# One early Silu on ScalarE, and the sum over h's squares one unit earlier, in a transformer block

## The chip, the cores and the metric

The kernel runs on one core of a Trainium2 chip. Its time is the device time of one execution in microseconds (us), as the median of several runs. The profile is that of one execution; its times count from the start of the span.

## The reference

A transformer block for 256 tokens of width 2048: an RMS norm, a projection into two attention branches with gates, the branches and their output product, and then the part that matters here, the second RMS norm and a gated feed-forward of width 5632:

```python
h = h + merged @ w_out[l]
hn = rms_norm(h, norm_ffn_g[l])          # h * rsqrt(mean(h*h) + eps) * g
h = h + (jax.nn.silu(hn @ w_ffn_gate[l]) * (hn @ w_ffn_up[l])) @ w_ffn_down[l]
```

All tensors are float32.

## The kernel before

Every product is taken in three passes. A matrix is split into a high half (a rounded copy, made by ScalarE) and a low half (the rest, made by VectorE), and TensorE sums high x high, low x high and high x low (L1593 to L1595). The products therefore need three engines in turn for each piece of a weight: SP's queue loads it, ScalarE makes `u_hi` (`unit_hi`, L946), VectorE makes `u_lo` (`unit_lo`, L1292), and TensorE multiplies (`product`).

The last quarter of the output product and the whole feed-forward run in units. A unit is a 512 x 512 piece of a weight (or a sum of such pieces), and a panel is the work for one pair of column blocks. In a "gu" panel these are 512 columns of the gate's product and the same of the up product. The first 1024 rows of a panel are multiplied with seven products in place of eight (M1 to M7, with sums and differences of quarters that VectorE forms: `sum_p` L1299, `sum_r` L1304, `sum_z` L1308). The other rows are plain units N0 to N3. An M unit has 12 matmuls, and an N or O unit has 24 (12 for each half of the tokens). N0 and N1 belong to the gate's half, N2 and N3 to the up half. The order is written out by hand:

```python
FIRST_ORDER = ("O0", "O1", "M1", "O2", "M5", "O3", "M6", "M2", "M7", "N0", "M3", "N1", "M4")
ORDER = ("M1", "N2-", "M5", "N3-", "M6", "M2", "M7", "N0", "M3", "N1", "M4")
```

The first line is panel 0, the second every later panel; "N2-" is unit N2 of the panel before. All engines walk the same list. Each of ScalarE and VectorE does the half of the unit and then what `first_unit` (panel 0) or `next_unit` (later panels) puts behind that unit. The high halves have four slots, three while panel 0 runs, and the low halves have three, so a unit's half can be made only when TensorE has used an older one.

The second norm's factor, `h_rs`, is a number for each token. It isn't applied to h ahead of the products but to their sums: `gate_opened` (L960) is a Silu of a gate bank with `h_rs` as its scale. It is made in these steps:

- ScalarE squares each quarter of h with a sum over its columns (`squares_of`, L1017), which raises `h_ss_ready`. The last quarter's squares stand behind N0's high half.
- VectorE adds the four sums (L1394, into `h_sum`) behind M4's low half of panel 0.
- GpSimd makes mean plus eps (`h_ms`, L729) and the power -0.5 (`h_rs`, L730). Its queue has the store of h's last quarter ahead of them and `sum_q` of panel 1 behind them (L756, a transfer that adds one quarter of a weight to another).

ScalarE's `gate_opened(panel 0, 0)` stands behind the high half of N2 in panel 1. It waits for the bank's last product (N1's first half) and for `h_rs`. TensorE's unit M1 of panel 1 writes into that same bank, and so has three waits: for its low half, for `gate_ready`, and for the operand:

```python
pe.wait_ge(lo_ready, u.index + 1)
...
elif before.kind == "gu":
    pe.wait_ge(gate_ready, T * before.col + 1)
...
left_ready(panel, 0)
```

ScalarE's functions need a table; the program has a table load (ACT_TABLE_LOAD) where a function is not in the loaded one. In the source no load is written; they come with the compilation. The kernel uses Copy, Square, Exp, Sigmoid (L867, L868) and Silu.

Of the kernel before, what the change touches and what calls it, by code (L numbers as in the profile page):

```python
# [23 lines left out]
ACT = mybir.ActivationFunctionType  # L24
# [3 lines left out]
P = 128  # L28
# [253 lines left out]
def build(nc, x, norm_mix_g, w_in, q_norm_a, k_norm_a, sink_a, t5_bias, q_norm_b, k_norm_b, rel_bias_b,  # L282
# [4 lines left out]
    NB = D // COLS  # L287
# [22 lines left out]
    with ExitStack() as ctx:  # L310
# [3 lines left out]
        def take(nbytes):  # L314
            offset = top[0]
            top[0] += nbytes + (-nbytes) % 32
            return offset

        def at(name, shape, dt, offset):
            return nc.alloc_sbuf_tensor_at(name, shape, dt, offset=offset)  # L320

        def sb(name, shape, dt=F32):
            return at(name, shape, dt, take(int(np.prod(shape[1:])) * 4))
# [71 lines left out]
        ident = sb("ident", [P, P])  # L395
# [9 lines left out]
        h_ss = sb("h_ss", [P, T, NB])  # L405
        h_sum = sb("h_sum", [P, T])
        h_ms = sb("h_ms", [P, T])
        h_rs = sb("h_rs", [P, T])
        q_ss = sb("q_ss", [P, T * NH])
        q_ms = sb("q_ms", [P, T * NH])  # L410
# [137 lines left out]
        def groups(n):  # L548
            return bass.ds(n * GROUP, GROUP) if not isinstance(n, int) else slice(n * GROUP, (n + 1) * GROUP)
# [228 lines left out]
        def _(act):  # L778
            A = nc.scalar.activation
# [28 lines left out]
            def scaled_to_hi(n):  # L808
                act.wait_ge(scaled_ready, n + 1)
                ts = 1 if n == 0 else T  # L810
                A(xT_hi[:, groups(n), :].rearrange("p k (t s) -> p t k s", t=T)[:, 0:ts],
                  staged[:].rearrange("p t (k s) -> p t k s", k=GROUP)[:, 0:ts], ACT.Copy).then_inc(scaled_hi, 1)
# [121 lines left out]
            def unit_hi(u):  # L934

                panel, slot = u.panel, u.panel.slot[u.raw]
                if u.name in ("M5", "M6", "M4"):
                    act.wait_ge(sum_ready, sums(panel, {"M5": "P", "M6": "R", "M4": "Z"}[u.name]))
                elif u.name == "M7":
                    act.wait_ge(q_summed, 16 * (panel.n + 1))  # L940
                else:
                    act.wait_ge(quad_landed[slot], panel.landed[u.raw])
                act.wait_ge(piece_used, u.hi_after)
                if u.hi == HI_SLOTS - 1:
                    act.wait_ge(xT_ready, KT // PIECE_KT + NB)
                A(u_hi[u.hi][:], quad[slot][:], ACT.Copy).then_inc(hi_ready, 1)  # L946
# [33 lines left out]
            def copy_m5(panel):  # L980

                act.wait_ge(piece_used, panel.unit["M5"].index + 1)
                if panel.n:
                    act.wait_ge(e_seeded, panel.n)
                A(m5, by_group(e_bank(panel)[:]), ACT.Copy).then_inc(m5_copied, 1)

            def copy_m1(panel):

                act.wait_ge(piece_used, panel.unit["M1"].index + 1)
                before = panel.prev  # L990
                if before is None:
                    act.wait_ge(h_ready, NB - 1)
                elif before.kind == "gu":
                    act.wait_ge(gate_ready, T * (before.col + 1))
                else:
                    act.wait_ge(evacuated0, T * (before.down + 1))
                A(b_bank(panel)[:], a_bank(panel)[:], ACT.Copy).then_inc(m1_copied, 1)
# [16 lines left out]
            def squares_of(n):  # L1014
                act.wait_ge(h_ready, n + 1)
                for t in range(T):
                    A(side_b[:, t, :], h[:, t, columns_of(n)], ACT.Square,  # L1017
                      accum_out=h_ss[:, t, n:n + 1]).then_inc(h_ss_ready, 1)

            def first_unit(u):  # L1020

                panel = panels[0]
                if u.name == "M6":
                    copy_m1(panel)
                if u.name == "M7":
                    copy_m5(panel)
                unit_hi(u)
                if u.name == "M1":
                    squares_of(NB - 2)
                if u.name == "M6":  # L1030
                    scaled_to_hi(NB - 2)
                if u.name == "N0":
                    squares_of(NB - 1)
                if u.name == "M3":
                    scaled_to_hi(NB - 1)

            def next_unit(panel, u):

                before = panel.prev
                if u.name == "M6":  # L1040
                    copy_m1(panel)
                if u.name == "M7":
                    copy_m5(panel)
                unit_hi(u)
                own = u.panel is panel
                if before.kind == "gu":
                    if u.name == "N2" and not own:
                        gate_opened(before, 0)
                    if u.name == "M5":
                        gate_opened(before, 1)  # L1050
                    if u.name == ("N1" if "N1" in panel.unit else "M4"):
                        hidden_hi(before)
                    if u.name == "M4" and before.block_slot == 1:
                        forms_hi(before)
                else:
                    if u.name == "N2" and not own:
                        evacuate(before, 0, 0)
                    if u.name == "M5":
                        evacuate(before, 0, 1)
                    if u.name == "M4":  # L1060
                        evacuate(before, 1, 0)
                        evacuate(before, 1, 1)
# [9 lines left out]
        def _(dve):  # L1072
# [27 lines left out]
            def scale_h(n, sets):  # L1100

                dve.wait_ge(turned, sets)
                if n:
                    dve.wait_ge(xT_ready, KT // PIECE_KT + n)
                g0 = KT + n * GROUP
                for t in range(T):
                    ins = V.tensor_tensor(by_group(staged[:, t, :]), by_group(bank[T_BANK + t][:]),
                                          g_col[:, g0:g0 + GROUP, None].to_broadcast([P, GROUP, P]), ALU.mult)
                ins.then_inc(scaled_ready, 1)
# [21 lines left out]
            def add_to_h(j, ready):  # L1131
                for t in range(T):
                    ins = V.tensor_tensor(h[:, t, columns(j)], bank[2 * j.pair + t][:], h[:, t, columns(j)], ALU.add)
                ins.then_inc(ready, 1)
# [154 lines left out]
            def unit_lo(u):  # L1289
                dve.wait_ge(hi_ready, u.index + 1)  # L1290
                dve.wait_ge(piece_used, u.lo_after)
                V.tensor_tensor(u_lo[u.lo][:], quad[u.panel.slot[u.raw]][:], u_hi[u.hi][:].bitcast(F32),  # L1292
                                ALU.subtract).then_inc(lo_ready, 1)

            def sum_p(panel):

                dve.wait_ge(quad_landed[panel.slot["12"]], panel.landed["12"])
                dst = quad[panel.slot["11"]][:]
                V.tensor_tensor(dst, dst, quad[panel.slot["12"]][:], ALU.add).then_inc(sum_ready, 1)  # L1299

            def sum_r(panel):
                dve.wait_ge(quad_landed[panel.slot["22"]], panel.landed["22"])
                dst = quad[panel.slot["11"]][:]
                V.tensor_tensor(dst, dst, quad[panel.slot["22"]][:], ALU.add).then_inc(sum_ready, 1)  # L1304
# [62 lines left out]
            def first_unit(u):  # L1367

                panel = panels[0]
                unit_lo(u)  # L1370
                if u.name == "O1":
                    dve.wait_ge(piece_used, PIECES)
                    add_to_h(jobs[-1], h_ready)
                if u.name == "M1":
                    sum_p(panel)
                if u.name == "M5":
                    sum_r(panel)
                if u.name == "O3":
                    scale_h(NB - 2, SETS - 1)
                if u.name == "M6":  # L1380
                    scaled_to_lo(NB - 2)
                if u.name == "M2":
                    add_last_to_h()
                if u.name == "M7":
                    seed_c(panel)
                if u.name == "N0":
                    scale_h(NB - 1, SETS)
                if u.name == "M3":
                    seed_e(panel)
                    scaled_to_lo(NB - 1)  # L1390
                    sum_z(panel)
                if u.name == "M4":
                    dve.wait_ge(h_ss_ready, T * NB)
                    V.tensor_reduce(h_sum[:], h_ss[:], AX.X, ALU.add).then_inc(h_sum_ready, 1)  # L1394

# [355 lines left out]
```

## Time and profile before

| | |
|---|---|
| median of 3 runs | 1291.85 us (1291.83 to 1291.9) |
| the profiled execution | 1291.89 us |
| its span | 1290.0 us |
| granted TensorE clock | 1.0 |
| busy: TensorE, weight load, VectorE, ScalarE, GpSimd | 99%, 82%, 74%, 55%, 5% |

The profiled execution's own time is 1.9 us more than the span, which counts from its first to its last instruction. TensorE's busy time includes the overlap of pipelined matmuls, so its pace is read from the starts of matmuls one after the other.

### The profile page before, as it was taken

The numbers are of one execution on the slowest core, as the hardware profiler recorded it, in microseconds if no ns is written. First come the engines' busy times: TensorE is split into PE (matmuls) and PEld (weight loads), VectorE is DVE, ScalarE is ACT, GpSimd is POOL, SyncE is SP. The second block draws the span as 40 slices with busy tenths as digits, with TensorE's granted clock in tenths as the row PEclk, the third lists the DMA queues.
The fourth block names the chain that finished last, engine by engine and source line by source line (L and its number), as shares of the span: only waits on it lengthen the run. The fifth ranks groups of instructions, "written<-read, shape, count | busy, mean of one in ns | idle before, by whom it ended". The sixth has DMA issues, their size and how long they took to land.

```text
span 1290.0 us, 15328 instructions
## 1 busy us (share of the span) xinstructions
PE 1283.5 (99%) x5996; PEld 1057.3 (82%) x5996; DVE 952.7 (74%) x919; ACT 709.5 (55%) x768; POOL 66.4 (5%) x65
## 2 busy tenths in 40 slices
PE   9999999999999999999999999999999999999999
PEld 7888887777788888888888888888888888888887
DVE  5655656777554555667898988888898878788996
ACT  5644445666554444455666655565565555565653
POOL 1221200000000000000100000000000001000000
DMA  8655376444466555676866687887957698866874
GB/s 296 224 170 194 131 238 207 152 151 151 162 238 193 178 185 195 211 248 192 290 215 217 192 260 230 253 244 220 293 200 227 194 276 256 252 225 196 276 218 125
DMA packets 136722, 276.55 MB, mean 214 GB/s; under 512 B 5248, under 2 KB 13760, under 8 KB 134224
## 3 DMA queue, kind: packets, MB, share of 16 engines
q1 hardware_dynamic: 130624, 250.37, 56.1%
q0 software_dynamic: 6032, 25.26, 10.4%
q8 instruction: 45, 0.74, 0.2%
q14 instruction: 21, 0.17, 0.0%
HBM read 249.38 MB, written 8.41 MB: 200 GB/s over the span
## 4 chain that ended last, share of the span: by engine, by line
PE 98%; ACT 1%; DVE 1%; DMA 0%; issue 0%; SPq 0%; ACTq 0%
PE bank L1593 18%; PE bank L1595 18%; PE bank L1594 18%; PE bank L1544 13%; PE bank L1546 13%; PE bank L1545 13%; PE bank L1492 1%; PE bank L1477 1%; PE bank L1517 1%; PE bank L1625 1%; PE bank L1502 1%; DMA x_rows<-in_x 0%; DVE u_lo L1292 0%; ACT prob L895 0%; PE bank L1519 0%
## 5 line engine op out<-in xcount | busy, mean ns | idle before, releaser
L1292 DVE TENSOR_TENSOR u_lo<-quad,u_hi 128x2048 fp32r<-128x2048 f32 x187 | 424.7, 2289 | 88.4 <-PE bank L1595 47.5
L946 ACT ACTIVATE u_hi<-quad 128x2048 fp32r<-128x2048 f32 x187 | 355.6, 1915 | 229.4 <-PE bank L1595 142.0
L1086 DVE TENSOR_TENSOR w_lo<-raw,w_hi 128x1024 fp32r<-128x1024 f32 (+1 forms) x192 | 229.6, 1202 | 190.4 <-ACT w_hi L791 188.2
L791 ACT ACTIVATE w_hi<-raw 128x1024 fp32r<-128x1024 f32 (+1 forms) x192 | 199.7, 1042 | 248.2 <-PE bank L1546 246.5
L1544 PE MATMUL bank<-w_hi,xT_hi 128*128 128x512 f32 (+1 forms) x544 | 213.7, 393 | 0.0
L1546 PE MATMUL bank<-w_lo,xT_hi 128*128 128x512 f32 (+1 forms) x544 | 208.8, 384 | 0.0
L1545 PE MATMUL bank<-w_hi,xT_lo 128*128 128x512 f32 (+1 forms) x544 | 208.6, 383 | 0.0
L1593 PE MATMUL bank<-u_hi,xT_hi 128*128 128x512 f32 x484 | 188.4, 389 | 0.7 <-DVE u_lo L1292 0.7
L1595 PE MATMUL bank<-u_lo,xT_hi 128*128 128x512 f32 x484 | 188.3, 389 | 0.0
L1594 PE MATMUL bank<-u_hi,xT_lo 128*128 128x512 f32 x484 | 188.3, 389 | 0.0
L1544 PEld LDWEIGHTS bank<-w_hi,xT_hi 128*128 128x128 f32 x544 | 102.3, 188 | 22.0 <-issue 1.0
L1546 PEld LDWEIGHTS bank<-w_lo,xT_hi 128*128 128x128 f32 x544 | 102.2, 188 | 20.7
L1545 PEld LDWEIGHTS bank<-w_hi,xT_lo 128*128 128x128 f32 x544 | 102.4, 188 | 18.3
L1593 PEld LDWEIGHTS bank<-u_hi,xT_hi 128*128 128x128 f32 x484 | 90.9, 188 | 19.9 <-DVE u_lo L1292 1.1
L1595 PEld LDWEIGHTS bank<-u_lo,xT_hi 128*128 128x128 f32 x484 | 90.9, 188 | 18.8
L1594 PEld LDWEIGHTS bank<-u_hi,xT_lo 128*128 128x128 f32 x484 | 90.9, 188 | 18.8
L1595 PE MATMUL bank<-u_lo,fT_hi 128*128 128x512 f32 (+1 forms) x236 | 91.0, 385 | 0.0
L1594 PE MATMUL bank<-u_hi,fT_lo 128*128 128x512 f32 (+1 forms) x236 | 91.0, 385 | 0.0
L1593 PE MATMUL bank<-u_hi,fT_hi 128*128 128x512 f32 (+1 forms) x236 | 91.0, 385 | 0.0
L1593 PE MATMUL bank<-u_hi,xs_hi 128*128 128x512 f32 x176 | 69.3, 394 | 0.0
L1595 PE MATMUL bank<-u_lo,xs_hi 128*128 128x512 f32 x176 | 68.6, 390 | 0.0
L1594 PE MATMUL bank<-u_hi,xs_lo 128*128 128x512 f32 x176 | 68.5, 389 | 0.0
(175 smaller groups left out, 1570.6 us busy)
## 6 DMA issues: line engine op xcount, KB each, us to landing
raw<-in_w_in SPq DMA_DIRECT2D x60, 1024.0 KB, 5.4
quad<-in_w_ffn_gate SPq DMA_DIRECT2D x44, 1024.0 KB, 7.0
quad<-in_w_ffn_up SPq DMA_DIRECT2D x44, 1024.0 KB, 6.1
quad<-in_w_ffn_down SPq DMA_DIRECT2D x44, 1024.0 KB, 6.4
quad<-quad POOLq DMA_DIRECT2D x17, 1024.0 KB, 8.2
raw<-in_w_out SPq DMA_DIRECT2D x12, 1024.0 KB, 5.1
raw<-in_w_branch_a SPq DMA_DIRECT2D x8, 1024.0 KB, 5.1
raw<-in_w_branch_b SPq DMA_DIRECT2D x8, 1024.0 KB, 5.1
```

The source lines that it names most:

```text
L791: A(w_hi[:, p % SPLIT_SLOTS, 0:w], raw[:, c % RAW_SLOTS, (p % 2) * w:(p % 2 + 1) * w], ACT.Copy).then_inc(hi_ready, 1)
L946: A(u_hi[u.hi][:], quad[slot][:], ACT.Copy).then_inc(hi_ready, 1)
L1086: V.tensor_tensor(w_lo[:, p % SPLIT_SLOTS, 0:w], raw[:, p // 2 % RAW_SLOTS, (p % 2) * w:(p % 2 + 1) * w], w_hi[:, p % SPLIT_SLOTS, 0:w].bi ...
L1292: V.tensor_tensor(u_lo[u.lo][:], quad[u.panel.slot[u.raw]][:], u_hi[u.hi][:].bitcast(F32), ALU.subtract).then_inc(lo_ready, 1)
L1477: ins = turn(bank[T_BANK + t][:, g * P:(g + 1) * P], src[:, t, g * P:(g + 1) * P], ident[:])
L1492: ins = M(dst, qT[rows, b * PAIRS + n, tokens(t)], k, start=True, stop=True)
L1544: M(sums, x_hi, w_hi[:, p % SPLIT_SLOTS, w], start=kt == 0, stop=False)
L1545: M(sums, x_lo, w_hi[:, p % SPLIT_SLOTS, w], start=False, stop=False)
L1546: ins = M(sums, x_hi, w_lo[:, p % SPLIT_SLOTS, w], start=False, stop=kt == j.kts - 1)
L1593: M(sums, a_hi(k), hi[:, w], start=start and k == 0, stop=False, skip_group_check=True)
L1594: M(sums, a_lo(k), hi[:, w], start=False, stop=False, skip_group_check=True)
L1595: ins = M(sums, a_hi(k), lo[:, w], start=False, stop=k == UNIT_KT - 1, skip_group_check=True)
```

## The change

ScalarE gets one more activation in `first_unit`, behind the high half of M3 and the copy of h's last transposed quarter: a Silu over four columns of the constant tile `ident` into a new tile `h_warm` that nothing reads. VectorE's sum over the four sums of squares, with its wait, moves from behind M4's low half to behind N1's, one unit earlier. The computed values are the same.

```diff
@@ -405,6 +405,7 @@
         h_ss = sb("h_ss", [P, T, NB])
         h_sum = sb("h_sum", [P, T])
         h_ms = sb("h_ms", [P, T])
+        h_warm = sb("h_warm", [P, NB])
         h_rs = sb("h_rs", [P, T])
@@ -1033,6 +1034,7 @@
                     squares_of(NB - 1)
                 if u.name == "M3":
                     scaled_to_hi(NB - 1)
+                    A(h_warm[:], ident[:, 0:NB], ACT.Silu)
 
@@ -1389,7 +1391,7 @@
                     seed_e(panel)
                     scaled_to_lo(NB - 1)
                     sum_z(panel)
-                if u.name == "M4":
+                if u.name == "N1":
                     dve.wait_ge(h_ss_ready, T * NB)
                     V.tensor_reduce(h_sum[:], h_ss[:], AX.X, ALU.add).then_inc(h_sum_ready, 1)
```

## Rows read from the trace of the kernel before

**Rows 1.** The page: busy time of each engine, and the chain's shares

```profile
PE 1283.5 (99%) x5996; PEld 1057.3 (82%) x5996; DVE 952.7 (74%) x919; ACT 709.5 (55%) x768; POOL 66.4 (5%) x65
...
PE 98%; ACT 1%; DVE 1%; DMA 0%; issue 0%; SPq 0%; ACTq 0%
```

**Rows 2.** Waits of TensorE: total us, times, longest us

```profile
PE bank L1593 <- DVE u_lo L1292: 0.7, 1, 0.7
```

**Rows 3.** Timeline of TensorE, 620 to 637 us: start, us, line, tiles, idle before

```profile
625.29 0.39 PE L1595 MATMUL bank<-u_lo,xs_hi 128*128 128x512 f32 x1
625.52 0.39 PE L1593 MATMUL bank<-u_hi,xT_hi 128*128 128x512 f32 x1
...
633.45 0.39 PE L1595 MATMUL bank<-u_lo,xT_hi 128*128 128x512 f32 x1
634.52 0.47 PE L1593 MATMUL bank<-u_hi,xT_hi 128*128 128x512 f32 x1 [0.68 <-DVE u_lo L1292]
...
635.06 0.39 PE L1595 MATMUL bank<-u_lo,xT_hi 128*128 128x512 f32 x1
```

**Rows 4.** Timeline of ScalarE, 590 to 662 us

```profile
614.20 0.19 ACT L1017 ACTIVATION_READ_ACCUMULATOR side_b<-h 128x1 f32 x1
...
616.80 1.06 ACT L811 ACTIVATE xT_hi<-staged 128x1024 fp32r<-128x1024 f32 x1 [0.61 <-DVE staged L1107]
617.77 1.90 ACT L946 ACTIVATE u_hi<-quad 128x2048 fp32r<-128x2048 f32 x1
623.06 5.53 ACT L946 ACTIVATE u_hi<-quad 128x2048 fp32r<-128x2048 f32 x3 [3.38 <-PE bank L1595]
632.44 1.28 ACT L960 ACT_TABLE_LOAD   x1 [3.85 <-POOL h_rs L730]
633.73 0.69 ACT L960 ACTIVATE side_a<-bank,h_rs 128x512 f32<-128x512 f32 x1
634.32 1.91 ACT L946 ACTIVATE u_hi<-quad 128x2048 fp32r<-128x2048 f32 x1
```

**Rows 5.** Timeline of VectorE, 590 to 662 us

```profile
620.62 2.29 DVE L1308 TENSOR_TENSOR quad<-quad,quad 128x2048 f32<-128x2048 f32 x1
622.82 4.49 DVE L1292 TENSOR_TENSOR u_lo<-quad,u_hi 128x2048 fp32r<-128x2048 f32 x2
627.23 0.16 DVE L1394 TENSOR_REDUCE h_sum<-h_ss 128x2 f32<-128x8 f32 x1
627.30 2.28 DVE L1292 TENSOR_TENSOR u_lo<-quad,u_hi 128x2048 fp32r<-128x2048 f32 x1
629.50 2.29 DVE L1299 TENSOR_TENSOR quad<-quad,quad 128x2048 f32<-128x2048 f32 x1
631.70 2.29 DVE L1292 TENSOR_TENSOR u_lo<-quad,u_hi 128x2048 fp32r<-128x2048 f32 x1
636.26 4.67 DVE L1292 TENSOR_TENSOR u_lo<-quad,u_hi 128x2048 fp32r<-128x2048 f32 x2 [2.28 <-ACT u_hi L946]
...
645.11 4.49 DVE L1292 TENSOR_TENSOR u_lo<-quad,u_hi 128x2048 fp32r<-128x2048 f32 x2 [1.98 <-ACT u_hi L946]
```

**Rows 6.** Timeline of GpSimd, 590 to 662 us

```profile
627.48 2.15 POOL L729 TENSOR_SCALAR h_ms<-h_sum 128x2 f32<-128x2 f32 x1 [16.68 <-DVE h_sum L1394]
629.72 2.65 POOL L730 TENSOR_TENSOR h_rs<-h_ms,minus_half 128x2 f32<-128x2 f32 x1
632.40 0.91 POOL L756 DMA_DIRECT2D quad<-quad  x1
```

**Rows 7.** Line 729 by itself: count, ns min/median/max, first and last start

```profile
L729 POOL TENSOR_SCALAR x_ms<-x_ss x1: 187/187/187, 36.3 to 36.3; 128x2 f32<-128x2 f32 x1
...
L729 POOL TENSOR_SCALAR h_ms<-h_sum x1: 2152/2152/2152, 627.5 to 627.5; 128x2 f32<-128x2 f32 x1
```

**Rows 8.** Timeline of ScalarE at the first Sigmoid, 340 to 400 us

```profile
358.45 1.28 ACT L867 ACT_TABLE_LOAD   x1
359.75 0.63 ACT L867 ACTIVATE gate_a<-gate_a 128x512 f32<-128x512 f32 x1
```

## Prediction

> **What bounds the kernel now.** I read the page first. TensorE is busy for 99% of the span, and the chain that ended last lies on TensorE for 98% of it [rows 1]. So a change on ScalarE, VectorE or GpSimd is worth only what it takes out of TensorE's idle time. The second view is that of TensorE's waits. After the first 10 us it lists one wait only, 0.7 us on L1593, put down to VectorE's u_lo [rows 2]. The third view is TensorE's timeline around that wait. Matmuls start every 0.227 us, and across a border of two units nothing is lost: the last matmul of M3 starts at 625.29 us and the first of N1 at 625.52 [rows 3]. N1 has 24 matmuls and M4 has 12, so the next unit, M1 of panel 1, is due at 625.52 + 36 x 0.2267 = 633.68 us. The last matmul of M4 does start on time, at 633.45. The first of M1 starts at 634.52, though, and the third at 635.06 instead of 633.45 + 3 x 0.227 = 634.13. TensorE therefore loses 635.06 - 634.13 = **0.93 us** here, and the steady pace after it wins nothing back. (The view of waits says 0.7, because it counts from the modelled end of the matmul ahead.)
>
> What did M1 of panel 1 wait for? The listed cause doesn't fit. VectorE's order after M3 is N1 and M4 (two u_lo from 622.82), the sum over the squares at 627.23, M1's u_lo from 627.30 to 629.58, sum_p, and then the u_lo from 631.70 to 633.99, which is that of N2, a unit later than M1 [rows 5]. M1's own low half was thus 4 us early. By the code, M1 also waits on gate_ready, that is, on the Silu of panel 0's first bank. ScalarE's timeline shows that Silu [rows 4]: its three u_hi (M4, M1, N2) end at 623.06 + 5.53 = 628.59, it sits idle for 3.85 us until h_rs is there, loads a table from 632.44 to 633.73, and runs the Silu to 633.73 + 0.69 = 634.42. TensorE starts 0.1 us later. The chain ahead of it is the edge of the matter: h_sum at 627.23, GpSimd's h_ms from 627.48 and h_rs from 629.72, ending at 632.37 [rows 6], the table load, the Silu.
>
> **The change part by part.** (1) *h_sum moves ahead of M4's low half.* It now stands behind N1's u_lo, which leaves VectorE at about 625.03 us. Its operands are there: the last read of an accumulator for the squares was at 614.20 and took 0.19 us [rows 4], so the moved wait holds nothing. VectorE's next instruction after h_sum started 0.07 us after it, so M4's u_lo starts at about 625.10 instead of 625.03 and ends at 627.4. TensorE wants it at 630.96 (625.52 + 24 x 0.2267), 3.5 us later. From M1's u_lo on, VectorE stands as before, since only the order changed.
>
> GpSimd has nothing queued ahead and starts h_ms as before 0.25 us after h_sum does, at 625.28, 2.2 us earlier. How long its pair takes there isn't shown, as other VectorE work runs beside it. For two columns the rows give 187 ns for x_ms early in the kernel and 2152 ns for h_ms [rows 6, 7]. h_ms ended at 629.63, just as the u_lo beside it did (629.58). In the new place it again starts within a u_lo (M4's, to 627.4), with M1's u_lo behind it. So I take the same pair, 627.48 to 632.37 or 4.89 us: h_rs at 625.28 + 4.89 = 630.17. As a low bound I take the 187 ns of x_ms and a second step no longer than now (2645 ns), giving 628.1; as a high bound one more blocked u_lo slot (2.2 us), giving 632.4. The Trainium skill, GPSIMD Engine Reference, section Key points, says that GpSimd shares its SBUF interfaces with VectorE and contends with VectorE instructions that have two SBUF inputs. By that rule the slow value is the right one here; by an undisturbed pair the result would be ready 2 to 4 us sooner, and the kernel's time by either would be the same.
>
> (2) *The early Silu.* It is issued on ScalarE after scaled_to_hi, whose activation ends at 617.86, and ahead of N1's u_hi, which now starts at 617.77 [rows 4]. It has no wait. The table load costs 1.28 us. At the Sigmoid, with no idle time ahead, one starts at 358.45 and the next activation at 359.75, so 1.30 us in all [rows 8]. A Silu of 4 columns isn't in the trace. Its bounds are the 0.19 us of the accumulator read (a single column) and the 0.69 us of a 512-column Silu [rows 4]; I take 0.2, the nearer. ScalarE is thus held for 1.5 us (at most 2.0), and N1's u_hi ends at 621.2 instead of 619.67. What hides it is VectorE's sum_z, which runs from 620.62 to 622.9 [rows 5], ahead of N1's u_lo at 622.82: no loss. If that cover were gone, the next deadline is TensorE's start of N1 at 625.52, less 2.3 us of u_lo and 0.1 for the handover, so 623.1. The early Silu may hold ScalarE for 3.4 us before TensorE sees it. The next u_hi, M4's, waits for TensorE until 623.06 anyway. Queued behind the early Silu are N1, M4, M1 and N2, all at their old times.
>
> (3) *The gate of panel 0.* Its Silu now starts when h_rs is there (630.17, with ScalarE free since 628.59) and its table is loaded, so it ends at 630.2 + 0.69 = 630.9. TensorE wants it at 633.68, and gate_ready is 2.8 us early. With the high bound of GpSimd it ends at 633.1, still ahead of TensorE. Either edit alone would do. Without the table load but with h_rs as now: 632.44 + 0.69 = 633.13, 0.5 us early. With h_rs at 630.2 but the load still there: 630.2 + 1.28 + 0.69 = 632.2, 1.5 us early. So the two together recover the 0.93 us once, not twice.
>
> (4) *What is late next.* TensorE then reaches N2 at 633.68 + 2.72 = 636.40; its u_lo ends at 633.99, unmoved: 2.4 us early. M5 follows at 636.40 + 5.44 = 641.84; before, its u_lo ran from 636.26 to 638.6, with ScalarE's u_hi behind the two Silus, and now that is earlier. M6, due at 650.0 (641.84 + 2.72 + 5.44), had its u_lo from 645.11 to 647.4 [rows 5]: 2.6 us early even if it didn't move. On GpSimd the accumulating transfer at 632.40 [rows 6] can go as soon as sum_p ends at 631.79, at most 0.6 us sooner, and on SP's queue the loads follow the low halves, some 2 us sooner at most. No new wait takes 0.93 us back.
>
> The sum: the profiled execution took 1291.89 us, span 1290.0. Less 0.93 that is 1290.96 and a span of 1289.1. The median shown is 1291.85, 0.04 below the profiled one, so I predict **1290.9 us**, 0.07% faster. A change of 0.2% would be 2.6 us, about the least that a measurement of this kernel tells from none, so by that bound nothing is seen.
>
> **The rivals.** *The listed cause is the true one:* TensorE waited for the u_lo that ended at 633.99. That instruction doesn't move, so the stall stays: 1291.85. For it speaks the view of waits [rows 2]; against it the 0.5 us between its end and TensorE's start, and the order of the units. *The change doesn't do what it says:* the early Silu's result is read by nobody and could be dropped, or GpSimd's work could be stretched so that h_rs is no earlier. One alone leaves the gate early, as in (3), and the time is 1290.9 again. Both together leave 1291.85. *A new wait takes part of it:* sooner loads and the sooner accumulating transfer crowd the queue while it is full, and one u_hi of panel 1 comes late by more than its 2.4 us of reserve. Giving back half of the gain would be 1291.4. *Slower:* the load on ScalarE in the middle of the panel makes N1's high half late. It decides from a hold of 3.4 us. At 4.3 the gain is gone, and at 4.3 + 2.6 = 6.9 us the kernel is 0.2% slower. Two loads and the Silu (2.8 us) would still be hidden; four (5.3 us) would cost 1.9 us: 1292.8. Against it: the trace has a single load for all 22 Silus and the copies between them, so Silu's table serves the copies. The Trainium skill, ScalarE: Activation LUTs, section What ACT_TABLE_LOAD costs, puts a switch at 1.28 us and 1.38 us of draining, 2.66 in all. The trace disagrees where it can, with 1.30 us from load to next activation; by the page the hold would be 2.9 us, with 0.5 us to spare instead of 1.9, and the sum the same.
>
> **How the numbers follow.** The full gain of 0.93 us, by both edits or by one, has 0.82; no change 0.08; a part of it 0.07; slower than before 0.03. Two builds may differ by some tenths without a cause in this chain, which I can't price from one trace. The range therefore runs from 0.3 below the likeliest time up to no change: 1290.6 to 1291.9. Faster by over 0.2% has 0.01, slower by over 0.2% has 0.02, and within it 0.97.
>
> **What the profile after would show.** The table load stands at about 617.9 us and not at the gate; three loads in all, as before. h_sum is at 625.0, h_rs ends near 630.2, and the first gate Silu runs at about 630.2. TensorE's wait at 634 is gone from the view of waits, and the first matmul of M1 starts at 633.7. The prediction is wrong if M1 still starts after 634, if N1 starts after 625.6, or if a wait of TensorE shows up in panel 1.

## The result and the profile after

The changed kernel takes **1294.59 us** (median of 20 executions, 1292.93 to 1294.95). The kernel before takes 1291.82 us (20 executions, 1291.33 to 1292.09). The ratio over all executions is 1.0018, 95% interval [1.0011, 1.0024] (that of the two medians is 1.0021): by the medians slower by 2.8 us, where 0.9 us faster was predicted. The executions fall into two groups. Seven lie at 1292.93 to 1293.00 with a mean granted clock of 1.0, thirteen at 1294.53 to 1294.95 with 0.999. The kernel before shows one group.

The page of the changed kernel reads as before [rows 1]: TensorE sets the time.

```profile
PE 1286.0 (99%) x5996; PEld 1059.5 (82%) x5996; DVE 952.6 (74%) x919; ACT 709.6 (55%) x769; POOL 71.0 (5%) x65
...
PE 98%; DVE 1%; issue 1%; POOL 0%; POOLq 0%; DVEq 0%
```

Beside TensorE's own busy time (1283.5 before), one figure has moved: GpSimd is busy for 71.0 us instead of 66.4. Its timeline, 590 to 662 us, shows where; [rows 6] answer to it.

```profile
625.26 8.76 POOL L730 TENSOR_SCALAR h_ms<-h_sum 128x2 f32<-128x2 f32 x1 [14.48 <-DVE h_sum L1396]
634.11 0.71 POOL L731 TENSOR_TENSOR h_rs<-h_ms,minus_half 128x2 f32<-128x2 f32 x1
634.79 0.90 POOL L757 DMA_DIRECT2D quad<-quad  x1
```

h_ms starts where it was expected, at 625.26, but lasts 8.76 us instead of 2.15. h_rs then takes 0.71 and ends at 634.82, 2.45 us *later* than before, although it started from a sum that was 2.2 us earlier. VectorE's timeline (624 to 640 us) stands beside it as [rows 5] did:

```profile
625.01 0.15 DVE L1396 TENSOR_REDUCE h_sum<-h_ss 128x2 f32<-128x8 f32 x1
625.08 4.48 DVE L1294 TENSOR_TENSOR u_lo<-quad,u_hi 128x2048 fp32r<-128x2048 f32 x2
629.49 2.28 DVE L1301 TENSOR_TENSOR quad<-quad,quad 128x2048 f32<-128x2048 f32 x1
631.69 2.28 DVE L1294 TENSOR_TENSOR u_lo<-quad,u_hi 128x2048 fp32r<-128x2048 f32 x1
637.43 2.29 DVE L1294 TENSOR_TENSOR u_lo<-quad,u_hi 128x2048 fp32r<-128x2048 f32 x1 [3.46 <-ACT u_hi L947]
```

Four instructions with two SBUF inputs run without a gap from 625.08 to 633.97, and h_ms ends at 634.02, as soon as VectorE stops. ScalarE's timeline, 590 to 662 us, shows that the early Silu did what it was put there for, and what it waited for later:

```profile
617.87 1.28 ACT L1037 ACT_TABLE_LOAD   x1
619.17 0.21 ACT L1037 ACTIVATE h_warm<-ident 128x4 f32<-128x4 f32 x1
619.28 1.91 ACT L947 ACTIVATE u_hi<-quad 128x2048 fp32r<-128x2048 f32 x1
623.05 5.53 ACT L947 ACTIVATE u_hi<-quad 128x2048 fp32r<-128x2048 f32 x3 [1.86 <-PE bank L1597]
634.91 0.69 ACT L961 ACTIVATE side_a<-bank,h_rs 128x512 f32<-128x512 f32 x1 [6.33 <-POOL h_rs L731]
```

The gate's Silu needs no load any more, and yet it ends at 635.60, because h_rs is late. TensorE's timeline around M1 of panel 1, which [rows 3] show for before:

```profile
633.44 0.39 PE L1597 MATMUL bank<-u_lo,xT_hi 128*128 128x512 f32 x1
635.70 0.67 PE L1595 MATMUL bank<-u_hi,xT_hi 128*128 128x512 f32 x1 [1.87 <-issue]
636.17 0.63 PE L1596 MATMUL bank<-u_hi,xT_lo 128*128 128x512 f32 x1
...
639.15 0.43 PE L1597 MATMUL bank<-u_lo,xT_hi 128*128 128x512 f32 x1
639.42 0.39 PE L1595 MATMUL bank<-u_hi,xT_hi 128*128 128x512 f32 x1
```

M1 starts at 635.70 instead of 634.52: 1.18 us lost against before. And its first matmuls start 0.43 us apart instead of 0.227. The windows of this profile (us; busy time of TensorE, weight load, VectorE, ScalarE, GpSimd; granted clock, DMA share, GB/s) say why:

```profile
633.67:635.70 2.03, 0.16 (x1) 0.03 (x1) 0.30 (x1) 0.79 (x2) 1.93 (x3) 1.00 0.98 288
635.70:639.42 3.72, 3.72 (x9) 2.91 (x10) 1.99 (x1) 3.72 (x3) 0.00 (x0) 0.54 1.02 307
639.42:645.00 5.58, 5.58 (x26) 4.64 (x25) 4.80 (x3) 1.04 (x3) 0.00 (x0) 1.00 0.94 190
```

Behind the pause the granted clock is 0.54 in the mean of 3.72 us, and 0.50 from 636.17 to 639.15: the lower of the two levels (1.2 GHz). At the pace before, the matmul that starts at 639.42 would have started 2.13 us behind 635.70 (0.31 and eight times 0.227), so this costs 3.72 - 2.13 = 1.59 us. Together 1.18 + 1.59 = 2.77 us, which is the difference of the medians (the spans differ by 1292.8 - 1290.0 = 2.8). The executions without the fall carry the 1.18 alone: 1292.97 - 1291.82 = 1.15.

### The profile page after: what moved, and what is told of

Read it like the earlier page. It is cut to its first block, busy times and chain, and to the rows that moved or that the text cites. A ratio compares the mean times of both kernels' runs of the same rounds, so it can differ in the third digit from the quotient of the medians.

```text
span 1292.8 us, 15329 instructions
## 1 busy us (share of the span) xinstructions
PE 1286.0 (99%) x5996; PEld 1059.5 (82%) x5996; DVE 952.6 (74%) x919; ACT 709.6 (55%) x769; POOL 71.0 (5%) x65
## 4 chain that ended last, share of the span: by engine, by line
PE 98%; DVE 1%; issue 1%; POOL 0%; POOLq 0%; DVEq 0%
PE bank L1595 17%; PE bank L1596 17%; PE bank L1597 17%; PE bank L1546 14%; PE bank L1548 13%; PE bank L1547 13%; PE bank L1494 1%; PE bank L1479 1%; PE bank L1504 1%; PE bank L1519 1%; PE bank L1627 1%; DVE u_lo L1294 1%; PE bank L1471 0%; PE bank L1464 0%; PE bank L1521 0%
```

## The experiments

All edits are against the changed kernel. The cuts of code show the lines that change and what stands beside them; where an edit puts the sum in a new place (e5, e6, e7), its two lines behind N1's low half are taken out. "Before" is the kernel before on the same chip, 1291.8 us throughout (1291.76 to 1291.83).

### One edit at a time

**e1**, the sum moved, no early Silu:

```diff
-                    A(h_warm[:], ident[:, 0:NB], ACT.Silu)
```

> Only the sum is moved; the early Silu is left out. Theory (GpSimd is held off while VectorE runs two-input work back to back): h_ms again lasts some 8.8 us, to about 634, h_rs ends at 634.8, then the table load (1.28) and the gate's Silu (0.69) come behind it, and TensorE's M1 starts at about 637.0 instead of 635.7. Time 1.3 us above the changed kernel's faster level of 1293.0, so 1294.2, or 1295.9 where the clock falls. Rival (the early Silu and its table load on ScalarE are what disturbs): h_rs at 630.2 as predicted, no stall, 1290.9.

Measured: 1295.89 us (6 executions, one at 1294.49 with the clock at 1.0, five at 1295.87 to 1296.98 with 0.997 to 0.999), ratio 1.0031 [1.0019, 1.0043]. GpSimd's and then ScalarE's timeline:

```profile
625.34 8.76 POOL L730 TENSOR_SCALAR h_ms<-h_sum 128x2 f32<-128x2 f32 x1 [14.48 <-DVE h_sum L1395]
```

```profile
634.97 1.28 ACT L961 ACT_TABLE_LOAD   x1 [6.32 <-POOL h_rs L731]
636.26 0.69 ACT L961 ACTIVATE side_a<-bank,h_rs 128x512 f32<-128x512 f32 x1
```

h_ms is as long without the early Silu, so the Silu is not the cause; the moved sum is, and the table load is 1.28 us more of the same wait. M1 starts at 637.05.

**e2**, the early Silu alone, the sum back behind M4:

```diff
-                if u.name == "N1":
+                if u.name == "M4":
                     dve.wait_ge(h_ss_ready, T * NB)
```

> Only the early Silu; the sum stays behind M4. Theory: GpSimd's pair is as before (h_rs ends at 632.4), the gate's Silu ends at 633.1, TensorE's M1 starts on time at 633.7, and the time is 1290.9, 0.93 below the kernel before. Rival (the early Silu disturbs): h_ms is long here too and the time is at or above 1293.

Measured: 1290.83 us (11 executions, 1290.52 to 1290.91), ratio 0.9992 [0.9983, 1.0001]. The interval takes in 1, but each of the 11 lies below each of before's 29 (lowest 1291.41). GpSimd's timeline, then ScalarE's:

```profile
627.45 2.15 POOL L730 TENSOR_SCALAR h_ms<-h_sum 128x2 f32<-128x2 f32 x1 [16.68 <-DVE h_sum L1396]
629.68 2.65 POOL L731 TENSOR_TENSOR h_rs<-h_ms,minus_half 128x2 f32<-128x2 f32 x1
```

```profile
632.42 0.69 ACT L961 ACTIVATE side_a<-bank,h_rs 128x512 f32<-128x512 f32 x1 [3.86 <-POOL h_rs L731]
```

The pair is what it was before. The gate's Silu ends at 633.11, TensorE's wait is gone, and the 0.93 us are back. This edit alone brings the whole gain that was predicted for both.

### Is it VectorE that holds GpSimd off?

**e3**, VectorE stands still behind the sum until h_rs is there:

```diff
                     V.tensor_reduce(h_sum[:], h_ss[:], AX.X, ALU.add).then_inc(h_sum_ready, 1)
+                    dve.wait_ge(h_rs_ready, 1)
```

> Both edits, and VectorE waits behind the sum until h_rs is there, so that GpSimd has a VectorE that stands still. Theory: h_ms takes 0.2 us and h_rs 0.7 us as for x at 36 us, h_rs ends at about 626.2, VectorE is 1.2 us later for M4, M1 and N2 (N2's low half ends at about 635.2, wanted at 636.4), TensorE doesn't stall, 1290.9. Rival (h_ms is slow in itself at this place, for instance because its code was last used at 186 us): VectorE stands still until 634 and M4's low half comes 6 us late: 1298 or more.

Measured: 1290.86 us (11 executions, 1290.50 to 1291.18), ratio 0.9993 [0.9984, 1.0002]. GpSimd's timeline and VectorE's next instruction:

```profile
625.52 0.19 POOL L730 TENSOR_SCALAR h_ms<-h_sum 128x2 f32<-128x2 f32 x1 [14.48 <-DVE h_sum L1396]
625.79 0.71 POOL L731 TENSOR_TENSOR h_rs<-h_ms,minus_half 128x2 f32<-128x2 f32 x1
```

```profile
626.54 4.50 DVE L1294 TENSOR_TENSOR u_lo<-quad,u_hi 128x2048 fp32r<-128x2048 f32 x2 [1.12 <-POOL h_rs L731]
```

The pair's own work is 0.98 us, in the same place, with the same operands and the same rest of the kernel. An idle VectorE for 1.1 us, which TensorE doesn't feel, turns 9.56 us of GpSimd into 0.98.

**e5** and **e6** place the sum earlier, ahead of VectorE work that reads a PSUM bank:

```diff
                 if u.name == "N0":
+                    dve.wait_ge(h_ss_ready, T * NB)
+                    V.tensor_reduce(h_sum[:], h_ss[:], AX.X, ALU.add).then_inc(h_sum_ready, 1)
                     scale_h(NB - 1, SETS)
```

> Both edits, with the sum placed earlier still: behind N0's low half, ahead of the two products that VectorE reads from a PSUM bank (scale_h, 1.28 us). Theory (only VectorE work with two SBUF inputs holds GpSimd off): h_ms takes about 0.2 us beside scale_h and h_rs 0.7 us, both end by 616.8, no stall of TensorE, 1290.9. Rival (any busy VectorE holds it off): h_ms lasts until VectorE's first idle time, near 634, as in the changed kernel, 1293.0 or 1294.6.

Measured: 1290.85 us (11 executions, 1290.50 to 1290.98), ratio 0.9992 [0.9983, 1.0001]. GpSimd's timeline:

```profile
615.68 0.19 POOL L730 TENSOR_SCALAR h_ms<-h_sum 128x2 f32<-128x2 f32 x1 [4.95 <-DVE h_sum L1390]
615.95 0.71 POOL L731 TENSOR_TENSOR h_rs<-h_ms,minus_half 128x2 f32<-128x2 f32 x1
```

VectorE was busy all the while, with scale_h (one input a PSUM bank) from 615.50 to 616.78, and GpSimd took no longer than beside an idle one. So it isn't any busy VectorE that holds it off, but the work in the row behind N1. That work has both inputs in SBUF, where scale_h has one in PSUM; it is also longer (2.28 us for each instruction, 0.68 us for each of scale_h's two), and no run has a long instruction with a single SBUF input in this place. e6 has the same two lines in M3, ahead of `seed_e`:

> Both edits, the sum behind M3's low half, ahead of seed_e (0.69 us, one input from PSUM) and of a long row of two-input SBUF work. Theory: h_ms gets through beside seed_e in about 0.2 us; h_rs starts 0.5 us later and isn't finished when the two-input work begins, so it is held off and may last until 634, with TensorE's stall back. Rival (a step once held off gets in at the next border of two VectorE instructions, as in the kernel before): h_rs ends by 622, no stall.

Measured: 1290.78 us (one execution). GpSimd's timeline, then VectorE's:

```profile
619.05 0.19 POOL L730 TENSOR_SCALAR h_ms<-h_sum 128x2 f32<-128x2 f32 x1 [8.34 <-DVE h_sum L1392]
619.32 0.71 POOL L731 TENSOR_TENSOR h_rs<-h_ms,minus_half 128x2 f32<-128x2 f32 x1
```

```profile
618.87 0.68 DVE L1326 TENSOR_TENSOR bank<-m,bank 128x512 f32<-128x512 f32 x1
619.46 1.22 DVE L1117 TENSOR_TENSOR xT_lo<-staged,xT_hi 128x1024 fp32r<-128x1024 f32 x1
```

I had expected h_rs to be held off here, and it wasn't: it started 0.14 us before xT_lo, which has two SBUF inputs, and ran to its end beside it. This step, once begun, was not stopped, in one execution. Nor was VectorE held by it: xT_lo took 1.22 us, as in the kernel before, and the next instruction started on time at 620.60.

### TensorE's clock

**e4** fills TensorE's pause with transposes of the constant tile into bank 7:

```diff
+                        if panel.n == 1:
+                            pe.wait_ge(scaled_ready, NB)
+                            spin(22)
                         pe.wait_ge(gate_ready, T * before.col + 1)
```

> The changed kernel, with 22 transposes of a constant tile into bank 7 on TensorE ahead of M1 of panel 1 (about 2.4 us of work that fills the stall). Theory (the granted clock fell because TensorE stood still for 2 us): M1's matmuls start every 0.227 us, no execution at the upper level, all near 1293.0 to 1293.4. Rival (the pace fell for another cause, such as the bank or the operands): some executions stay at 1294.6 and the spacing of 0.43 us is still there.

Measured: 1293.29 us (11 executions, 1292.97 to 1293.49, clock 1.0 in all), ratio 1.0011 [1.0002, 1.002]. TensorE's timeline:

```profile
633.36 2.56 PE L1471 MATMUL bank<-ident 128*128 128x128 f32 x22
635.68 0.47 PE L1595 MATMUL bank<-u_hi,xT_hi 128*128 128x512 f32 x1
635.99 0.39 PE L1596 MATMUL bank<-u_hi,xT_lo 128*128 128x512 f32 x1
```

The wait for the gate is the same and the upper group is gone. (All times of this profile are 0.3 us lower than in that of the changed kernel: M4's last matmul starts at 633.13, so M1 starts 2.55 us behind it, where it was 2.26.) That 0.3 us more, also in the median over 1292.97, is the transposes' own end, which outlasts the gate's Silu (to 635.29). So the 1.6 us belong to the pause, not to M1's operands.

### What opens the way within the row

**e8** puts a memset of an unused tile on VectorE between the low halves of M4 and M1:

```diff
                 unit_lo(u)
+                if u.name == "M4":
+                    V.memset(inv[:], 0.0)
```

> The changed kernel with one small memset of an unused tile on VectorE between the low halves of M4 and M1. Theory (GpSimd needs an opening between two-input instructions, and this is one): h_ms ends at about 627.5 and h_rs by 632, no stall, 1290.9. Rival (a short instruction of another kind opens nothing): h_ms still lasts 8.8 us, 1293.0 or 1294.6.

Measured: 1290.88 us (10 executions, 1290.70 to 1290.97), ratio 0.9992 [0.9983, 1.0002]. GpSimd's timeline:

```profile
625.23 2.15 POOL L730 TENSOR_SCALAR h_ms<-h_sum 128x2 f32<-128x2 f32 x1 [14.48 <-DVE h_sum L1398]
627.47 2.65 POOL L731 TENSOR_TENSOR h_rs<-h_ms,minus_half 128x2 f32<-128x2 f32 x1
```

The memset is in VectorE's timeline:

```profile
627.28 0.07 DVE L1374 MEMSET inv<- 128x8 f32 x1
```

One instruction of 0.07 us brings 8.76 us down to 2.15, and with that the prediction's own picture: h_rs ends at 630.12. **e9**, **e10** and **e11** put the opening at a later border, which the held-off h_ms of the changed kernel didn't get through: one memset behind M1's low half (629.5 us), six there, and one behind sum_p (631.7 us).

```diff
                 if u.name == "M1":
+                    if panel.n == 1:
+                        V.memset(inv[:], 0.0)
                     sum_p(panel)
```

> The changed kernel, with the small memset one border later than in the run that had it behind M4's low half: behind M1's low half, at 629.5 us, where the changed kernel's h_ms (started at 625.3) did not get in. Theory (a memset between two of these instructions is an opening whenever it comes): h_ms ends at about 629.6, h_rs at 631.8 to 632.5, the gate is on time, 1290.9. Rival (a step that missed its first border is held off until VectorE stops, whatever stands at the later borders): h_ms ends at 634.1 as in the changed kernel, 1293.0 or 1294.6.

> As the one before with six memsets of unused tiles at that border, some 0.3 to 0.5 us without two-input work. Theory (the length of the opening counts): h_ms ends there, at about 629.8, even if one memset wasn't enough. Rival (only an idle VectorE lets it in after a miss): h_ms ends near 634.4.

> The changed kernel with one memset at the third border, behind sum_p at 631.7. Theory (any opening): h_ms ends at about 631.8, h_rs at 634.7, gate late as before: 1292.8 to 1294.6. Rival: h_ms ends at 634.1, h_rs at 634.9.

Measured, one execution each: 1290.86, 1290.62 and 1292.76 us. h_ms in e9 and in e11, from GpSimd's timelines:

```profile
625.25 4.36 POOL L730 TENSOR_SCALAR h_ms<-h_sum 128x2 f32<-128x2 f32 x1 [14.48 <-DVE h_sum L1396]
```

```profile
625.27 6.56 POOL L730 TENSOR_SCALAR h_ms<-h_sum 128x2 f32<-128x2 f32 x1 [14.48 <-DVE h_sum L1396]
```

h_ms ends at 629.61 and at 631.83, each time right behind the memset, and six memsets do no more than one (4.35 us). They made no wider opening than that either: they overlap and take 0.15 us together (629.23 to 629.38) and not the 0.3 to 0.5 expected, so e10 doesn't test the opening's length. The rival, that a step that missed a border stays out whatever comes, is refuted. In e11 the gate is late for the reason foreseen: h_rs asks at 631.91 and ends at 634.57.

**e12** puts a small add with two SBUF inputs (8 columns) where e8 has its memset:

```diff
+                if u.name == "M4":
+                    V.tensor_tensor(inv[:], denom[:], row_sum[:], ALU.add)
```

> The changed kernel with a small add of two SBUF tiles (8 columns) on VectorE between the low halves of M4 and M1, where the memset stood in an earlier run. Theory (what holds GpSimd off is an unbroken row of instructions with two SBUF inputs): this one has two such inputs, so nothing opens, h_ms lasts 8.8 us, 1293.0 or 1294.6. Rival (what is closed is only the border between two like u_lo, and any other instruction between them opens it): h_ms ends at about 627.5, 1290.9.

Measured: 1292.78 us (10 executions, 1292.49 to 1292.98, clock 1.0 in all), ratio 1.0008 [0.9998, 1.0017]. GpSimd's timeline:

```profile
625.34 2.18 POOL L730 TENSOR_SCALAR h_ms<-h_sum 128x2 f32<-128x2 f32 x1 [14.48 <-DVE h_sum L1398]
627.60 7.11 POOL L731 TENSOR_TENSOR h_rs<-h_ms,minus_half 128x2 f32<-128x2 f32 x1
```

VectorE's:

```profile
627.36 0.17 DVE L1374 TENSOR_TENSOR inv<-denom,row_sum 128x8 f32<-128x8 f32 x1
627.45 2.28 DVE L1294 TENSOR_TENSOR u_lo<-quad,u_hi 128x2048 fp32r<-128x2048 f32 x1
```

Neither expectation holds as it stood. The time is the theory's, but h_ms got in at the add, which the theory excludes. Two SBUF inputs alone are therefore not what closes the way; the small add has them too. Then h_rs was held off for 7.1 us, over the borders at 629.65 and 631.85, of the same kinds as those at which h_rs got in before [rows 5, 6] and in e8.

**e13 to e15** shift the moment at which a step asks, by small adds: one (e13) or three (e14) between the sum and M4's low half, two at e12's place (e15).

> The changed kernel with one small two-input add between the sum and M4's low half, which starts that u_lo some 0.09 us later against h_ms's request. Theory M (the moment of the request decides): h_ms's length is no longer 8.76 us, it gets in at the first border, 627.5. Theory K (the kinds of the instructions at the border decide; u_lo followed by u_lo is closed): h_ms is still held off to 634.

> As before with three small adds, some 0.3 us: h_ms has room to end ahead of M4's low half (in about 0.2 to 0.3 us, near 625.5) if short instructions let it in, and h_rs asks some 0.2 us into that u_lo. Theory M: h_rs may get in at any border. Theory K: the first border (u_lo to u_lo) is closed to h_rs, and as a step that missed a border it stays out until 634.

> The run with one small add at the first border, now with two. With one add h_rs asked 0.15 us into M1's low half and lasted 7.1 us; with the memset there it asked 0.22 us into it and lasted 2.65 us. Theory M: with another moment (asked up to 0.1 us before to 0.1 us into that u_lo) the length is a different one. Theory K: the same instructions stand at the later borders, so h_rs lasts until 634 again.

Measured, one execution each: 1294.31, 1294.54 and 1292.93 us. h_ms lasts 8.83 us in e13 and 8.99 in e14; in e15 it lasts 2.17 and h_rs 7.19. No shift opened anything. For e13 this is what theory K had said, and theory M is refuted as it was put there. e14 didn't come to its question: the adds ahead of M4's low half gave h_ms no room (it starts at 624.94, the third add at 624.91, the u_lo at 624.99), so it was h_ms and not h_rs that was held off. In e15 h_rs again lasted until VectorE stopped, as K had said and M had not; why these borders were closed to it at all, K doesn't say.

**e7** has the sum one unit later than before, behind M1's low half of panel 1, ahead of sum_p:

```diff
                 unit_lo(u)
+                if u.name == "M1" and panel.n == 1:
+                    dve.wait_ge(h_ss_ready, T * NB)
+                    V.tensor_reduce(h_sum[:], h_ss[:], AX.X, ALU.add).then_inc(h_sum_ready, 1)
```

> Both edits, the sum one unit later than in the kernel before, behind M1's low half of panel 1; sum_p and N2's low half follow, then idle time from 634. Theory A (each step gets in at the next border): h_ms ends at about 631.9, h_rs at about 634.6. Theory B (a step held off stays so until VectorE stops): h_ms ends at 634.1 and h_rs at 634.9. In either the gate is late and TensorE's M1 starts near 635.5: 1292.8 to 1294.6.

Measured: 1292.68 us (one execution), h_ms 2.15 us from 629.63, h_rs 2.64 from 631.86, so it ends at 634.50 and the gate is late. This is theory A's course, in this place: the changed kernel's h_ms passed three borders.

## Why the prediction was wrong

**What bounded the kernel** was read rightly. That M1 of panel 1 waited for the gate's Silu and not for the listed u_lo is shown by e2, where that u_lo stays (631.66 to 633.94), the Silu ends 1.3 us sooner and the wait is gone. The loss of 0.93 us is shown too: e2, e3, e5 and e8 measure 1290.83 to 1290.88, 0.92 to 1.00 below the kernel before on the same chip. The rival "the listed cause is the true one" is out.

**The early Silu** went as worked out: load at 617.87, 1.30 us to the Silu, 0.21 us for that (0.2 taken), N1's high half to 621.2, no loss. Its slower rival, a hold of over 3.4 us, had a hold of 1.5.

**The time** lies outside the range of 1290.6 to 1291.9, and the sign that was given for a wrong prediction, M1 starting after 634, is there (635.70).

**The step that failed** is in part (1): "So I take the same pair, 627.48 to 632.37 or 4.89 us", with "one more blocked u_lo slot" as the high bound. The pair took 625.26 to 634.82, or 9.56 us; the bound had been 7.1. The start, the moved sum and M4's low half (625.08) were right to 0.03 us. The fault is in the reading of [rows 6, 7]. They showed 2152 ns for a step whose own work is 187, and I treated the rest as a property of the pair. The contention with VectorE was named there, but its length was carried over from the old place. For the second step the same trace has, in the view of line 730 by itself:

```profile
L730 POOL TENSOR_TENSOR x_rs<-x_ms,minus_half x1: 719/719/719, 36.6 to 36.6; 128x2 f32<-128x2 f32 x1
```

x_ms and the start of x_rs fall into idle time of VectorE, which has nothing to do until 37.17. So the excess of both steps, 4.89 - 0.19 - 0.72 = 4.0 us, could be read off before. It was a wait for VectorE, as e3 shows (0.19 and 0.71 us with VectorE standing still), and a wait has to be worked out from what stands in the row behind it in the new place. [Rows 5] had that row: from the moved sum to VectorE's next idle time at 633.99 there are four two-input instructions without a gap. The high bound was therefore 634.0, plus 0.2 and 0.7 for the pair and 0.69 for the Silu: M1 at 635.6 (measured 635.70), over 1 us later than before. It was the rival on the other side, and it wasn't among mine; the slower one that I gave lay on ScalarE and never came near.

**"Either edit alone would do"** in part (3) failed with it. The Silu alone does (e2: 1290.83). The moved sum alone costs 4 us (e1: 1295.89). And the early Silu takes 1.3 us off that, the table load (1295.89 - 1294.59 = 1.30).

**The clock** was left out. A pause can cost more than its length: with one of 2.26 us between two starts of matmuls, 13 of 20 executions lost 1.6 us more, and none did with the pause filled (e4). That is the larger part of the 2.8.

**Still open** is what decides whether a step gets in at a border of two of the long instructions. Take the step's start in the profile as the moment at which it asks. Where it asked 0.17 to 0.22 us into the running instruction and the next border was that of a u_lo and a sum_p, it got in (before, e2, e7, e8, e9). At the border of two u_lo it didn't (changed kernel, e1, e4, e9 to e11). Where it asked 0.07 to 0.15 us into a u_lo or just ahead of one (h_ms in e13 and e14, h_rs in e12 and e15), it got in at no border of two long instructions. But e10 has a step that asked as early and got in at the next one:

```profile
629.42 2.73 POOL L731 TENSOR_TENSOR h_rs<-h_ms,minus_half 128x2 f32<-128x2 f32 x1
```

```profile
629.29 2.28 DVE L1301 TENSOR_TENSOR quad<-quad,quad 128x2048 f32<-128x2048 f32 x1
631.49 2.28 DVE L1294 TENSOR_TENSOR u_lo<-quad,u_hi 128x2048 fp32r<-128x2048 f32 x1
```

It asked 0.13 us into sum_p and ended at 632.15, 0.66 us behind the border, as before. So the moment of asking alone doesn't decide: 0.13 (e10) got in and 0.15 (e12) didn't, and 0.18 is in both groups (before, changed kernel). The kinds at the border alone don't either: h_rs in e12 missed those that let it in before. Whether the two act together, or something else does, no run shows. Shown is only this much: a short instruction that came while a step waited, or idle time, let it in each time.

## What to carry to other kernels

Take a GpSimd step's duration apart before moving it: compare it with the same step beside an idle VectorE, and take the rest as a wait whose length the new place sets. Hand GpSimd its work ahead of VectorE work that reads PSUM or of a wait of VectorE, not ahead of a row of long two-input SBUF instructions; an earlier start there can give a later end. And when an upper bound for a wait is wanted, run the row of the engine that causes it to its next gap.

## What the runs showed of the hardware

- The GpSimd step h_ms, over 2 columns, lasts 0.19 us beside an idle VectorE (e3) or one that reads PSUM (e5, e6), 2.15 us where it gets in at the first border, and up to 8.99 us (e14) beside a row of long VectorE instructions with two SBUF inputs. The Trainium skill, SBUF — State Buffer, section SBUF: two separate sides, has this as an exclusive lock on a shared port pair that the one who starts first holds for its instruction. The traces agree in that GpSimd is blocked and that a step of its own that has begun runs on (e6). They don't show the other side, VectorE blocked: xT_lo took 1.22 us beside h_rs and as much without it. And the blocking did not end with the instruction: three borders passed in the changed kernel without letting GpSimd in.
- A memset of 0.07 us on VectorE between two such instructions lets a waiting step in (e8, e9, e11), and so does an add of 8 columns (e12).
- TensorE's clock, by gap between two starts of matmuls at M1: 1.07 us (kernel before), none of the 65 executions beside the runs with less than clock 1.0; 1.98 (e7), 2.00 (e11) and 2.15 us (e15), not in the one execution of each; 2.08 us (e12), none of 10; 2.26 us (changed kernel), 13 of 20; 2.34 (e13) and 2.49 us (e14), in the one of each; 3.54 us (e1), 5 of 6. The gaps are those of the profiled executions, and the runs were on several chips; e13 to e15 shared one. With the gap filled by transposes (e4) none of 11. In the changed kernel's profile the granted clock is 0.50 from 636.17 to 639.15 and 1.00 again from 639.42.
- The table load took 1.28 us, and the next activation began 1.30 us after the load's start, with ScalarE busy up to the load.
